# Packing the 16-row leftovers of a hybrid attention block into TensorE column groups

## The chip, the cores and the metric

One NeuronCore of one Trainium2 chip (trn2). The metric is the device time of one execution in microseconds; lower is better. The kernel is one program on one core, and everything is float32.

## The reference, cut to what matters

A decoder block: layer norm of 16 meta tokens and 2048 real tokens, then two groups of heads side by side (4 retention heads of 128, 8 forgetting-attention heads of 64), an output projection, and a mixture of 64 experts. Only the real tokens are returned.

```python
h = concatenate([meta, x])                      # 16 + 2048 = 2064 rows of 1024
h = layer_norm(h, ln0_g, ln0_b)
proj = h @ w_in                                 # rq, rk, rv, rg (4 x 128 each), fq, fk, fv (8 x 64), ff (8)
logf = log_sigmoid(ff + b_forget)
ret  = retention(rotary(rq), rotary(rk) * 128 ** -0.5, rv)      # in chunks of 128, state carried over
ret  = head_norm(ret) * silu(rg)
fox  = forgetting_attention(fq, fk, fv, logf)   # softmax(q k / 8 + c_q - c_k), c = cumsum(logf)
h = layer_norm(ALPHA * h + concatenate([ret, fox]) @ w_out, ...)
# then the mixture of experts and the last norm
```

2064 rows are sixteen blocks of 128 and 16 rows over. Two parts of the kernel meet such a leftover of 16 rows: the forgetting attention's values `fv`, in blocks from row 0, whose last block has 16 rows; and each retention head, whose first chunk is the 16 meta rows, for which only keys and values are needed (for the state), no queries and no gate.

## The kernel before, in words

The program runs in stages on one core. The **embedding stage** (`embed_phase`) normalises the rows, transposes them to `hT` (1024 features as 8 chunks of 128 partitions, 2064 columns), and on the way projects the values block by block (`values(b)`, lines 447 to 455): 8 matmuls, one for each feature chunk, stationary `hT` (128 x rows), moving the weights `wv` (128 x 512). For the last block, `b == NB - 1`, there are 16 stationary columns, and the result stands in partitions 0 to 15 of PSUM bank 7. TensorE's order at the end is: `forget()` (lines 457 to 469), `values(15)`, `values(16)`. `forget()` projects the 8 forget gates for 2048 rows in four matmuls per chunk, each of 512 rows, whose outputs start at partitions 0, 32, 64 and 96. ScalarE copies the values to SBUF (`copy_v`, line 410), and SyncE stores them to `v_rows` (line 287). ScalarE and VectorE make the gates out of `forget()`'s result: lines 366 to 380 on VectorE, 402 and 404 on ScalarE; SyncE stores the sums as `ck` (line 285), and only then, in its queue, the last value block. ScalarE copies value blocks 15 and 16 behind its part of the gates.

Then comes **retention** (`retention_phase`), a hardware loop of two rounds with two heads each. TensorE waits before its loop for the copy of value block 15 (`v_copied` at 16) and for the forget copies; ScalarE waits before its loop for all stores of the embedding stage. In a head, TensorE's `project(m)` (line 704) makes queries, keys, values and gates of chunk m (m = 0: the 16 meta rows, keys and values only, 256 columns; m > 0: 128 rows, 512 columns), in two PSUM banks by turns; ScalarE's `evacuate(m)` (lines 598 to 603) copies them out, VectorE's `rotate(m)` (lines 638 to 642) applies the rotary factors to queries and keys, and TensorE's `outer(m)` (line 714) multiplies rotated keys with weighted values into the state. The order at the start of a head is written out by hand:

```python
project(0)
project(1)
outer(0)      # waits for rotate(0)
project(2)
for n in range(NX): ...
```

After its 16 chunks a head is normalised: POOL takes the reciprocal root, VectorE subtracts and scales (line 677, 16 instructions) and multiplies with the gates (line 682), and only after that, in its program order, rotates chunk 0 of the next head. The forgetting attention (`fox_phase`) and the expert stage (`moe_phase`) follow. The attention's product of weights and values (line 1120) writes two heads to partitions 0 to 63 and 64 to 127 of one bank.

In SBUF the copy's tiles `vst` (values), `qk` (queries and keys), `vz` (weighted values) and `r` (rotated) exist twice, by turns.

Of the kernel before, what the change touches and what calls it, by code (L numbers as in the profile page):

```python
# [14 lines left out]
P = 128  # L15
D = 1024
DC = D // P
SEQ = 2048
NX = SEQ // P
META = 16  # L20
TOK = META + SEQ
NB = -(-TOK // P)
# [174 lines left out]
def embed_phase(nc, ps, ident, hT, square, x, meta, ln_g, ln_b, ln_gcol, ln_bcol, w_in, b_forget, h_rows, v_rows, ck, rope, retc, ahead):  # L197


    with Phase(nc, "emb") as ph:  # L200
# [194 lines left out]
        @block.scalar  # L395
        def _(act):
            act.wait_ge(const, 48)

            def softplus(k):
                lo, hi, _ = CUT[k]  # L400
                act.wait_ge(gate, k + 1)
                nc.scalar.activation(t2[:, lo:hi], t1[:, lo:hi], ACT.Exp).then_inc(gate_e, 1)
                act.wait_ge(gate_e, k + 1)
                nc.scalar.activation(t1[:, lo:hi], t2[:, lo:hi], ACT.Ln, bias=1.0).then_inc(gate_a, 1)

            def copy_v(b):
                act.wait_ge(v_done, b + 1)
                if b >= 2:
                    act.wait_ge(v_out[b % 2], 16 * (b // 2))
                nc.scalar.copy(vst[b % 2][0:vrows[b], :], ps[0:vrows[b], 7 if b == NB - 1 else 4 + b % 2, :]).then_inc(v_copied, 1)  # L410

            for i in range(NT):
                r = rows[i]
                act.wait_ge(turned, i + 1)
                for c in range(4):
                    ins = nc.scalar.activation(hT[:, c, tok0[i]:tok0[i] + r],
                                               ps[:, 2 * (i % 2), c * P:c * P + r], ACT.Identity,
                                               bias=bcol[:, c:c + 1], scale=gcol[:, c:c + 1])
                ins.then_inc(hT_a, 1)
                if i >= 2:  # L420
                    copy_v(i - 2)
            act.wait_ge(const_r, 48)
            for k, (o, n) in enumerate(FCH):
                act.wait_ge(f_done, 1 if n == BANK else 2)
                bank = ps[32 * k:32 * k + FH, 6, :] if n == BANK else ps[0:FH, 7, :]
                nc.scalar.activation(z[:, o:o + n], bank[:, 0:n], ACT.Identity, bias=bf[:, 0:1]).then_inc(f_copied, 1)
            softplus(0)
            copy_v(NT - 2)
            copy_v(NT - 1)

        @block.tensor
        def _(pe):
            def turn(i):
                r = rows[i]
                pe.wait_ge(normed, i + 1)
                if i >= 2:
                    pe.wait_ge(hT_a, i - 1)
                    pe.wait_ge(hT_d, i - 1)
                for c in range(DC):
                    ins = pe.transpose(ps[:, 2 * (i % 2) + c // 4, (c % 4) * P:(c % 4) * P + r],  # L440
                                       xn[i % 2][0:r, c * P:(c + 1) * P], ident[0:r, 0:r])
                ins.then_inc(turned, 1)

            def values(b):

                pe.wait_ge(hT_a, min(b + 2, NT))
                pe.wait_ge(hT_d, min(b + 2, NT))
                if b == NB - 1:
                    pe.wait_ge(f_copied, len(FCH))
                elif b >= 2:  # L450
                    pe.wait_ge(v_copied, b - 1)
                for c in range(DC):
                    ins = pe.matmul(ps[0:vrows[b], 7 if b == NB - 1 else 4 + b % 2, :], hT[:, c, P * b:P * b + vrows[b]], wv[:, c, :],
                                    start=(c == 0), stop=(c == DC - 1))
                ins.then_inc(v_done, 1)

            def forget():
                pe.wait_ge(wf_in, 16)
                pe.wait_ge(hT_a, NT)
                pe.wait_ge(hT_d, NT)  # L460
                for c in range(DC):
                    for k in range(4):
                        ins = pe.matmul(ps[32 * k:32 * k + FH, 6, :], wf[:, c, :], hT[:, c, BANK * k:BANK * (k + 1)],
                                        start=(c == 0), stop=(c == DC - 1))
                ins.then_inc(f_done, 1)
                for c in range(DC):
                    ins = pe.matmul(ps[0:FH, 7, 0:TOK - 4 * BANK], wf[:, c, :], hT[:, c, 4 * BANK:TOK],
                                    start=(c == 0), stop=(c == DC - 1))
                ins.then_inc(f_done, 1)

            pe.wait_ge(const, 48)
            for i in range(NT):
                turn(i)
                if i == 2:
                    pe.wait_ge(wv_in, 16)
                if i >= 2:
                    values(i - 2)
            forget()
            values(NT - 2)
            values(NT - 1)  # L480
# [3 lines left out]
def retention_phase(nc, ps, ident, hT, square, w_in, retc, v_rows, ck, mixed, ahead):  # L484


    with Phase(nc, "ret") as ph:
# [85 lines left out]
        @block.scalar  # L573
        def _(act):

            for sem_, n_ in ahead.rows_out:
                act.wait_ge(sem_, n_)
            act.wait_ge(w_in_s[0], 80 + START)
            with act.Fori(0, RH // 2) as j:
                for u in range(2):  # L580
                    def evacuate(m):

                        b, n = (u + m) % 2, META if m == 0 else P
                        bank = ps[0:n, b, :]
                        act.wait_ge(proj, (j * 2 + u) * NM + m + 1 + START)

                        if m == 2:
                            act.wait_ge(state_mm, (j * 2 + u) * NX + 1 + START)
                        if m >= 3:
                            act.wait_ge(att, (j * 2 + u) * NX + m - 2 + START)  # L590
                        if m == 0:
                            act.wait_ge(w_in_s[u], j * 80 + 80 + START)

                            act.wait_ge(att, (j * 2 + u) * NX + START)
                            act.sem_inc(spare[0], 1)
                        zeta = rc[u][0:n, P + 3:P + 4] if m == 0 else rc[u][:, P:P + 1]
                        if m > 0:
                            nc.scalar.activation(qk[b][:, 0:RD], bank[:, 0:RD], ACT.Copy, scale=rc[u][:, P + 1:P + 2])
                            nc.scalar.copy(v[b][:, :], bank[:, 2 * RD:3 * RD])
                        nc.scalar.copy(qk[b][0:n, RD:2 * RD], bank[:, RD:2 * RD])  # L600
                        ins = nc.scalar.activation(vz[b][0:n, :], bank[:, 2 * RD:3 * RD], ACT.Copy, scale=zeta)
                        if m > 0:
                            ins = nc.scalar.activation(sg[u][:, m - 1, :], bank[:, 3 * RD:4 * RD], ACT.Silu)
                        ins.then_inc(evac, 1)


                    act.wait_ge(mix_out[u], j * 16 + START)
                    act.sem_inc(spare[0], 1)
                    evacuate(0)
                    evacuate(1)  # L610
                    evacuate(2)
                    for n in range(NX):
                        m = n + 1
                        act.wait_ge(turned, (j * 2 + u) * NX + n + 1 + START)
                        nc.scalar.copy(rT[n % 2][:, :], ps[:, 2, 0:2 * RD]).then_inc(turned_c, 1)
                        act.wait_ge(att, (j * 2 + u) * NX + n + 1 + START)
                        nc.scalar.copy(ret[u][:, n, :], ps[:, 4 + n % 2, 0:RD]).then_inc(out_c, 1)
                        if m + 2 < NM:
                            evacuate(m + 2)
# [66 lines left out]
        def _(pe):  # L686
            pe.wait_ge(ahead.v_copied[0], ahead.v_copied[1] - 1)
            pe.wait_ge(*ahead.f_copied)
            with pe.Fori(0, RH // 2) as j:
                for u in range(2):  # L690
                    def project(m):
                        n, t0 = (META, 0) if m == 0 else (P, META + P * (m - 1))
                        b = (u + m) % 2
                        lo, hi = (RD, 3 * RD) if m == 0 else (0, 4 * RD)
                        if m < 2:

                            if u == 1:
                                pe.wait_ge(evac, (j * 2 + u) * NM + m - 1 + START)
                            else:
                                pe.wait_ge(evac, j * (2 * NM) + START)  # L700
                        else:
                            pe.wait_ge(evac, (j * 2 + u) * NM + m - 1 + START)
                        for c in range(DC):
                            ins = pe.matmul(ps[0:n, b, lo:hi], hT[:, c, t0:t0 + n], wr[u][:, c, lo:hi],  # L704
                                            start=(c == 0), stop=(c == DC - 1))
                        ins.then_inc(proj, 1)
# [1610 lines left out]
```

## Time and profile before

| | us |
|---|---|
| median of 3 runs | 3263.11 (3262.07 to 3263.48) |
| the profiled execution | 3265.91 |
| its span, first to last instruction | 3264.1 |
| TensorE busy | 3111.6 (95%) |
| VectorE, ScalarE, GpSimd busy | 1105.6, 693.6, 635.4 |
| mean granted TensorE clock | 0.982 |

How to read it. TensorE is `PE`, its weight loads `PEld`; VectorE is `DVE`, ScalarE `ACT`, GpSimd `POOL`, SyncE's DMA queue `SPq`. A row of a timeline gives start, length, engine, line, operation, what is written and read (partitions x elements), how many records in a row, and in brackets how long the engine stood idle before it and what ended that. An fp32 matmul leaves two records. The length of a merged row runs to the end of its last record, which overlaps the next row a little; the spacing of records is therefore taken from starts. `128*16 128x256` is a stationary tile of 128 partitions by 16 columns, and a moving tile of 256 columns. The granted clock is 1.00 at 2.4 GHz and 0.50 at 1.2 GHz.

### The profile page before, as it was taken

To read this page: it belongs to the slowest core of one execution; us is meant where nothing else is said; L and a number is where in the kernel's file an instruction comes from. 1 tells how busy PE (TensorE), PEld (TensorE's weight loads), DVE (VectorE), ACT (ScalarE), POOL (GpSimd) and SP (SyncE) were. 2 spreads that over 40 slices of the span, in tenths; PEclk is the share of its full clock that TensorE was granted. 3 is DMA by queue.
4 is the path that set the end of the run, shared out by engine and by line. 5 is a ranking of instruction groups with operands and counts; after the bars stand their busy time and mean duration, and the time that the engine had idled before them with its cause. 6 is when DMAs were issued, how large, how long until landed. Compare 5 with 4: busy or idle time off the path is not lost.

```text
span 3264.1 us, 38644 instructions
## 1 busy us (share of the span) xinstructions
PE 3111.6 (95%) x14302; PEld 1998.4 (61%) x14302; DVE 1105.6 (34%) x3356; ACT 693.6 (21%) x1547; POOL 635.4 (19%) x623
## 2 busy tenths in 40 slices
PE   8999999999999899898999999999999999999991
PEld 4444545454445555554556767778777778787771
DVE  6423333330035656663777331111111111111115
ACT  2221111110024454451111001111111111111114
POOL 3200000000000010101444202222222222223224
PEclk9999999999999999999999999999999999999996
DMA  6421010001000102005334467788888888888886
GB/s 227 139 66 40 1 41 1 14 12 47 20 1 8 48 9 104 11 8 179 130 123 139 140 226 210 230 238 239 233 245 244 242 240 258 261 263 270 271 262 226
DMA packets 179985, 462.06 MB, mean 142 GB/s; under 512 B 25040, under 2 KB 97568, under 8 KB 154056
## 3 DMA queue, kind: packets, MB, share of 16 engines
q1 hardware_dynamic: 134736, 342.38, 29.8%
q0 software_dynamic: 42752, 108.72, 15.2%
q10 hardware_dynamic: 2304, 8.39, 0.6%
q8 instruction: 120, 1.97, 0.2%
q14 instruction: 73, 0.60, 0.1%
HBM read 345.47 MB, written 113.92 MB: 141 GB/s over the span
## 4 chain that ended last, share of the span: by engine, by line
PE 52%; DVE 1%; DMA 0%; POOL 0%; ACT 0%; issue 0%; SPq 0%; POOLq 0%; ACTq 0%; DVEq 0%
PE ps L2229 22%; PE ps L2167 11%; PE ps L2053 7%; PE ps L2151 4%; PE ps L2099 3%; PE ps L2111 2%; PE ps L2164 2%; PE ps L2073 1%; PE ps L2063 0%; POOL moe_fin L1904 0%; DMA moe_fin<-base_rows 0%; DVE moe_fin L1617 0%; PE ps L2040 0%; DMA base_rows<-moe_yo,index 0%; DVE moe_shift L1612 0%
## 5 line engine op out<-in xcount | busy, mean ns | idle before, releaser
L704 PE MATMUL ps<-ret_w,hT 128*128 128x512 f32 (+1 forms) x1088 | 467.9, 584 | 3.2 <-issue 3.2
L2229 PEld LDWEIGHTS ps<-moe_xT,moe_wg 128*128 128x128 f32 x2048 | 352.6, 196 | 44.8 <-issue 40.8
L2229 PE MATMUL ps<-moe_xT,moe_wg 128*128 128x192 f32 (+22 forms) x2048 | 378.4, 338 | 0.0
L2229 PE MATMUL ps<-moe_xT,moe_wu 128*128 128x192 f32 (+22 forms) x2048 | 375.3, 336 | 0.0
L2167 PE MATMUL ps<-moe_wd,moe_hh 128*128 128x512 f32 (+12 forms) x800 | 366.5, 601 | 1.0 <-DVE moe_hh L1433 0.8
L2229 PEld LDWEIGHTS ps<-moe_xT,moe_wu 128*128 128x128 f32 x2048 | 353.3, 196 | 4.3
L704 PEld LDWEIGHTS ps<-ret_w,hT 128*128 128x128 f32 (+1 forms) x1088 | 196.2, 185 | 229.7 <-issue 224.1
L1840 POOL DMA_INDIRECT base_rows<-moe_yo,index x100 | 164.8, 1648 | 848.0 <-DVE moe_yo L1535 680.5
L1433 DVE TENSOR_TENSOR moe_hh<-moe_sl,ps 128x256 f32<-128x256 f32 (+19 forms) x144 | 53.8, 374 | 797.4 <-ACT moe_sl L1934 797.3
L2167 PEld LDWEIGHTS ps<-moe_wd,moe_hh 128*128 128x128 f32 (+12 forms) x800 | 136.6, 181 | 159.4 <-issue 149.8
L1058 PE MATMUL ps<-hT,fox_w 128*128 128x512 f32 (+1 forms) x576 | 228.4, 558 | 0.0
L1934 ACT ACTIVATE moe_sl<-ps 128x256 f32<-128x256 f32 (+19 forms) x144 | 49.9, 346 | 791.0 <-PE ps L2229 652.2
L910 DVE CUSTOM_DVE_ANT_0 hT<-ps,fox_c 128x512 f32<-128x512 f32 (+7 forms) x320 | 166.3, 560 | 124.5 <-PE ps L1069 124.3
L887 POOL TENSOR_TENSOR fox_diag<-fox_c,fox_causal 128x128 f32<-128x128 f32 x128 | 55.8, 458 | 700.4 <-DVE fox_mx L916 700.0
L1058 PEld LDWEIGHTS ps<-hT,fox_w 128*128 128x128 f32 x576 | 105.2, 191 | 123.3 <-issue 123.3
L1535 DVE TENSOR_SCALAR moe_yo<-ps,weight 128x512 f32<-128x512 f32 x100 | 75.0, 750 | 302.3 <-PE ps L2167 302.3
L1088 PE MATMUL ps<-ident,hT 128*128 128x128 f32 (+1 forms) x1024 | 150.7, 282 | 24.5 <-ACT hT L1011 11.1
L1011 ACT ACTIVATE hT<-hT,fox_nm 128x1936 f32<-128x1936 f32 (+15 forms) x128 | 155.0, 1212 | 69.0 <-DVE fox_nm L925 68.7
L1088 PEld LDWEIGHTS ps<-ident,hT 128*128 128x128 f32 (+1 forms) x1024 | 107.5, 137 | 87.1 <-issue 63.3
L1819 POOL DMA_INDIRECT moe_xg<-t_rows,index x129 | 129.7, 1006 | 145.7 <-DMA base_rows<-moe_yo 69.5
L2151 PEld LDWEIGHTS ps<-ident,moe_xg 128*128 128x128 f32 (+14 forms) x1032 | 131.2, 196 | 40.5 <-issue 40.1
L1113 PE MATMUL ps<-fox_pT,fox_v 128*64 128x256 f32 (+2 forms) x1088 | 144.3, 382 | 3.2 <-DVE fox_pT L938 2.8
(246 smaller groups left out, 3587.8 us busy)
## 6 DMA issues: line engine op xcount, KB each, us to landing
moe_wg<-in_we_gate SPq DMA_DIRECT2D x64, 1024.0 KB, 5.0
moe_wu<-in_we_up SPq DMA_DIRECT2D x64, 1024.0 KB, 7.1
moe_wd<-in_we_down SPq DMA_DIRECT2D x64, 1024.0 KB, 7.8
fox_c<-ck SPq DMA_DIRECT2D x8, 1032.0 KB, 8.6
emb_xin<-in_x SPq DMA_DIRECT2D x16, 512.0 KB, 3.7
h_rows<-emb_hr SPq DMA_DIRECT2D x16, 512.0 KB, 2.8
ret_w<-in_w_in SPq DMA_DIRECT2D x16, 512.0 KB, 6.6
moe_yt<-h_rows SPq DMA_DIRECT2D x16, 512.0 KB, 4.9
```

The costliest lines, as they stand in the source:

```text
L704: ins = pe.matmul(ps[0:n, b, lo:hi], hT[:, c, t0:t0 + n], wr[u][:, c, lo:hi], start=(c == 0), stop=(c == DC - 1))
L910: ins = dve.tensor_tensor_reduce(out=row[:, lo:m], in0=bank[:, 0:m - lo], in1=negc[p % 2][:, a, lo:m], scale=1.0, scalar=NEG, op0=ALU.add, ...
L1011: nc.scalar.activation(row, row, ACT.Exp, bias=nm[(2 * n + q) % 4][:, a:a + 1], accum_out=rs[n % 2][:, r:r + 1]).then_inc(exped, 1)
L1058: ins = pe.matmul(ps[:, x % 8, 0:n], wqk[job % 2][:, c, :], hT[:, c, tok:tok + n], start=(c == 0), stop=(c == DC - 1))
L1088: ins = pe.transpose(ps[0:hi - lo, T0 + g % 2, P * r:P * (r + 1)], prob[n % 2][2 * q + a][:, lo:hi], ident[:, :])
L1113: ins = pe.matmul(ps[FD * a:FD * (a + 1), O0 + n % 2, P * q0:QT], vp[p % 2][0:m, st, FD * a:FD * (a + 1)], pT[g % 4][0:m, 2 * a + q0:2 * a ...
L1819: pool.indirect_dma_start(out=xg[r][0:n, :], out_offset=None, in_=t_rows, in_offset=bass.IndirectOffsetOnAxis(ap=route.index[0:n, k * NE + ...
L1840: pool.indirect_dma_start(out=base_rows, out_offset=bass.IndirectOffsetOnAxis(ap=route.index[0:n, c:c + 1], axis=0), in_=yo[r][0:n, :], in ...
L2053: ins = pe.matmul(ps[:, 2 + a, :], mT[i % 2][:, c, :] if c < RH else fT[i % 2][:, c - RH, :], wo[:, c, a * BANK:(a + 1) * BANK], start=(c ...
L2151: ins = pe.transpose(ps[:, h, c * P:c * P + n], xg[g % NXG][0:n, 4 * h + c:D:DC], ident[0:n, 0:n])
L2167: ins = pe.matmul(ps[0:n, bank + h, :], hh[i % 2][:, f, k * P:k * P + n], rhs, start=(f == 0), stop=(f == FC - 1))
L2229: ins = pe.matmul(out, w[:, c, f:FF:FC], xT[u][:, c, 0:n], start=(c == 0), stop=(c == DC - 1))
```

## The change

The values of the last 16 rows are made in four column groups: for each feature chunk four matmuls of 128 weight columns each, whose outputs start at partitions 0, 32, 64 and 96 of bank 7, and ScalarE gathers them with four copies. The keys of the 16 meta rows are made apart from their values: keys go to partitions 32 to 47 of the bank, values stay at 0 to 15, two matmuls of 128 columns in place of one of 256; ScalarE reads the keys from there. No wait, no DMA and no other instruction is changed.

```diff
@@ embed_phase, ScalarE: copy_v
-                nc.scalar.copy(vst[b % 2][0:vrows[b], :], ps[0:vrows[b], 7 if b == NB - 1 else 4 + b % 2, :]).then_inc(v_copied, 1)
+                if b < NB - 1:
+                    ins = nc.scalar.copy(vst[b % 2][0:vrows[b], :], ps[0:vrows[b], 4 + b % 2, :])
+                else:
+                    for g in range(4):
+                        ins = nc.scalar.copy(vst[b % 2][0:vrows[b], P * g:P * (g + 1)],
+                                             ps[32 * g:32 * g + vrows[b], 7, P * g:P * (g + 1)])
+                ins.then_inc(v_copied, 1)
@@ embed_phase, TensorE: values
+                n = vrows[b]
                 for c in range(DC):
-                    ins = pe.matmul(ps[0:vrows[b], 7 if b == NB - 1 else 4 + b % 2, :], hT[:, c, P * b:P * b + vrows[b]], wv[:, c, :],
-                                    start=(c == 0), stop=(c == DC - 1))
+                    rows_c = hT[:, c, P * b:P * b + n]
+                    if b < NB - 1:
+                        ins = pe.matmul(ps[0:n, 4 + b % 2, :], rows_c, wv[:, c, :], start=(c == 0), stop=(c == DC - 1))
+                    else:
+                        for g in range(4):
+                            ins = pe.matmul(ps[32 * g:32 * g + n, 7, P * g:P * (g + 1)], rows_c, wv[:, c, P * g:P * (g + 1)],
+                                            start=(c == 0), stop=(c == DC - 1))
                 ins.then_inc(v_done, 1)
@@ retention_phase, ScalarE: evacuate
-                        nc.scalar.copy(qk[b][0:n, RD:2 * RD], bank[:, RD:2 * RD])
+                        keys = bank if m > 0 else ps[32:32 + META, b, :]
+                        nc.scalar.copy(qk[b][0:n, RD:2 * RD], keys[:, RD:2 * RD])
@@ retention_phase, TensorE: project
-                        lo, hi = (RD, 3 * RD) if m == 0 else (0, 4 * RD)
+                        hi = 3 * RD if m == 0 else 4 * RD
...
                         for c in range(DC):
+                            if m == 0:
+                                pe.matmul(ps[32:32 + n, b, RD:2 * RD], hT[:, c, t0:t0 + n], wr[u][:, c, RD:2 * RD],
+                                          start=(c == 0), stop=(c == DC - 1))
+                            lo = 2 * RD if m == 0 else 0
                             ins = pe.matmul(ps[0:n, b, lo:hi], hT[:, c, t0:t0 + n], wr[u][:, c, lo:hi],
                                             start=(c == 0), stop=(c == DC - 1))
```

In TensorE's program, from the last value blocks to the first wait of the second stage, this stood before (each row one instruction or a run of them; shapes are the output's):

```order
L453 MATMUL ps<-emb_wv,hT 128x512 [waits emb_v_copied0,emb_hT_d0,emb_hT_a0]
L453 MATMUL ps<-emb_wv,hT 128x512 x7
L453 MATMUL ps<-emb_wv,hT 16x512 [waits emb_f_copied0,emb_hT_d0,emb_hT_a0]
L453 MATMUL ps<-emb_wv,hT 16x512 x7
L685 UNCONDITIONAL_BRANCH
L689 UNCONDITIONAL_BRANCH [waits emb_f_copied0,emb_v_copied0]
L689 ISA
L700 ISA [waits ret_ret_w0]
L704 MATMUL ps<-ret_w_52,hT 16x256 [waits ret_evac]
L704 MATMUL ps<-ret_w_52,hT 16x256 x7
L704 MATMUL ps<-ret_w_52,hT 128x512 [waits ret_evac]
```

and this now:

```order
L465 MATMUL ps<-emb_wv,hT 16x128 [waits emb_f_copied0,emb_hT_d0,emb_hT_a0]
L465 MATMUL ps<-emb_wv,hT 16x128 x31
L698 UNCONDITIONAL_BRANCH
L702 UNCONDITIONAL_BRANCH [waits emb_f_copied0,emb_v_copied0]
L702 ISA
L713 ISA [waits ret_ret_w0]
L718 MATMUL ps<-ret_w_52,hT 16x128 [waits ret_evac]
L721 MATMUL ps<-ret_w_52,hT 16x128
L718 MATMUL ps<-ret_w_52,hT 16x128
L721 MATMUL ps<-ret_w_52,hT 16x128
```

Eight matmuls of 512 columns became 32 of 128, and eight of 256 became 16 of 128, keys and values by turns; the waits stand where they stood.

In ScalarE's program, at the end of the embedding stage, before:

```order
L404 ACTIVATE emb_t_92<-emb_t_93 8x2064 [waits emb_gate_e0]
L410 COPY emb_vst_81<-ps 128x512 [waits emb_v_out1,emb_v_done0]
L410 COPY emb_vst_80<-ps 16x512 [waits emb_v_out0,emb_v_done0]
L573 UNCONDITIONAL_BRANCH
L579 UNCONDITIONAL_BRANCH [waits emb_v_out1,emb_v_out0,emb_c_out0,emb_h_out1,ret_ret_w0,emb_h_out0,emb_hrow0]
```

and now:

```order
L404 ACTIVATE emb_t_92<-emb_t_93 8x2064 [waits emb_gate_e0]
L411 COPY emb_vst_81<-ps 128x512 [waits emb_v_out1,emb_v_done0]
L414 COPY emb_vst_80<-ps 16x128 [waits emb_v_out0,emb_v_done0]
L414 COPY emb_vst_80<-ps 16x128 x3
L585 UNCONDITIONAL_BRANCH
L591 UNCONDITIONAL_BRANCH [waits emb_v_out1,emb_v_out0,emb_c_out0,emb_h_out1,ret_ret_w0,emb_h_out0,emb_hrow0]
```

One copy became four; the wait for the stores still follows them.

## Rows read from the trace of the kernel before

**Rows 1.** the page: busy times, and the granted TensorE clock in 40 slices
```profile
PE 3111.6 (95%) x14302; PEld 1998.4 (61%) x14302; DVE 1105.6 (34%) x3356; ACT 693.6 (21%) x1547; POOL 635.4 (19%) x623
...
PEclk9999999999999999999999999999999999999996
```

**Rows 2.** timeline, TensorE, 132 to 166 us: start, length, line, operation [idle before]
```profile
132.94 7.05 PE L463 MATMUL ps<-hT,emb_wf 128*8 128x512 f32 x64
139.81 0.56 PE L467 MATMUL ps<-hT,emb_wf 128*8 128x16 f32 x16
140.29 14.11 PE L453 MATMUL ps<-emb_wv,hT 128*128 128x512 f32 x32
154.23 10.68 PE L704 MATMUL ps<-ret_w,hT 128*16 128x256 f32 x32
165.49 0.48 PE L714 MATMUL ps<-ret_vz,ret_r 16*128 16x128 f32 x2 [0.58 <-DVE ret_r L642]
```

**Rows 3.** timeline of ScalarE, 150 to 166 us
```profile
150.63 0.56 ACT L410 COPY emb_vst<-ps 128x512 f32<-128x512 f32 x1
...
162.41 1.28 ACT L600 ACT_TABLE_LOAD   x1 [7.40 <-DMA v_rows<-emb_vst]
...
163.86 0.35 ACT L601 ACTIVATE ret_vz<-ps,ret_rc 16x128 f32<-16x128 f32 x1
```

**Rows 4.** timeline of SyncE's DMA queue, 150 to 166 us
```profile
158.82 0.29 SPq L285 DMA_DIRECT2D ck<-emb_t  x1
159.15 0.32 SPq L287 DMA_DIRECT2D v_rows<-emb_vst  x1
```

**Rows 5.** timeline of VectorE, 150 to 166 us
```profile
157.57 1.22 DVE L380 TENSOR_SCALAR emb_t<-emb_t 8x2064 f32<-8x2064 f32 x1
...
165.15 0.21 DVE L642 TENSOR_TENSOR ret_r<-ret_cosd,ret_sind 16x64 f32<-16x64 f32 x1
```

**Rows 6.** timeline of TensorE, 1374 to 1380 us, in the forgetting attention
```profile
1378.20 1.09 PE L1120 MATMUL ps<-fox_pT,fox_v 128*64 128x128 f32 x16
1379.23 1.13 PE L1069 MATMUL ps<-fox_k,fox_q 64*128 64x512 f32 x4
```

**Rows 7.** timeline of TensorE, 286 to 316 us, into the second head
```profile
293.76 11.39 PE L704 MATMUL ps<-ret_w,hT 128*16 128x256 f32 x32
306.07 0.48 PE L714 MATMUL ps<-ret_vz,ret_r 16*128 16x128 f32 x2 [0.92 <-DVE ret_r L642]
```

**Rows 8.** timeline of VectorE, 286 to 316 us, the same place
```profile
302.73 2.29 DVE L682 TENSOR_TENSOR ret_ret<-ret_ret,ret_sg 128x2048 f32<-128x2048 f32 x1
```

**Rows 9.** timeline of TensorE, 578 to 591 us, into the fourth head
```profile
578.06 10.69 PE L704 MATMUL ps<-ret_w,hT 128*16 128x256 f32 x32
590.28 0.48 PE L714 MATMUL ps<-ret_vz,ret_r 16*128 16x128 f32 x2 [1.53 <-DVE ret_r L642]
```

**Rows 10.** timeline of TensorE, 437 to 451 us, into the third head
```profile
437.67 12.80 PE L704 MATMUL ps<-ret_w,hT 128*16 128x256 f32 x32 [3.16 <-issue]
450.40 0.48 PE L714 MATMUL ps<-ret_vz,ret_r 16*128 16x128 f32 x2
```

**Rows 11.** timeline of VectorE, 443 to 448 us, the same place
```profile
443.34 2.29 DVE L682 TENSOR_TENSOR ret_ret<-ret_ret,ret_sg 128x2048 f32<-128x2048 f32 x1
...
447.28 0.21 DVE L642 TENSOR_TENSOR ret_r<-ret_cosd,ret_sind 16x64 f32<-16x64 f32 x1
```

**Rows 12.** timeline of TensorE, 1484 to 1512 us, at the start of the MoE phase
```profile
1499.19 1.09 PE L2040 MATMUL ps<-ident,moe_mix 128*128 128x128 f32 x4 [5.81 <-PEq L145]
```

**Rows 13.** windows: stretch, its length, busy time of each engine, PEclk, DMA share, GB/s
```profile
291.70:295.10 3.40, 3.24 (x10) 1.94 (x11) 1.05 (x5) 0.37 (x2) 0.15 (x1) 0.51 0.07 10
...
431.70:441.90 10.20, 6.58 (x19) 2.91 (x18) 4.14 (x17) 0.91 (x3) 3.21 (x2) 0.50 0.65 168
...
1499.20:1506.90 7.70, 7.03 (x11) 3.20 (x12) 1.18 (x10) 0.59 (x1) 4.41 (x7) 0.50 0.83 260
...
588.70:597.00 8.30, 6.77 (x18) 3.25 (x18) 3.00 (x14) 1.13 (x5) 0.00 (x0) 1.00 0.43 126
```

## The prediction

> **What bounds the kernel now.** I read the page first: TensorE is busy 95% of the span, with the granted clock full nearly throughout [rows 1]. So TensorE time that is saved normally comes off the end; the question is whether it is saved where TensorE is the engine others wait for. The change sits in five places only: the last 16 value rows, and the 16 meta rows at the start of each of the four heads. I then read, for each of the five, the TensorE timeline and whatever ends TensorE's next wait.
>
> *Into the first head.* TensorE ends the forget projections, then does the last two value blocks (32 records from 140.29; the last 16 are the 16-row block), the meta rows' projection and the first 128 rows' projection (32 records from 154.23), and then stops for 0.58 us before the first state product, outer(0), at 165.49 [rows 2]. What ends that stop is a chain that does not begin at TensorE's late work: VectorE finishes the gate sums at 158.79; SyncE issues the store of ck and then, behind it, the store of the last 16 value rows (159.15) [rows 4, 5]; ScalarE stands 7.40 us until that store has landed, loads its table at 162.41 and copies the meta rows' keys and values by 164.21 [rows 3]; VectorE rotates the keys by 165.36 [rows 5]; outer(0) follows. The gate sums depend on the forget projections, which come before everything the change touches.
>
> *Into the second and fourth heads.* TensorE stops again in front of outer(0), 0.92 and 1.53 us, for the rotated keys [rows 7, 9]. VectorE is late there because it still finishes the previous head: the gating multiply ends at 302.73 + 2.29 = 305.02 and the rotation can only follow [rows 8].
>
> *Into the third head* it is the other way round: the keys are ready at 447.49, and TensorE reaches outer(0) at 450.40 without a stop [rows 10, 11]. Here TensorE is the late one, by 2.9 us.
>
> **The change, part by part.** An fp32 matmul is two records in this trace, so 8 matmuls of 512 columns are 16 records.
>
> *Values of the last 16 rows.* Before: (154.23 − 140.29) / 32 = 0.436 us a record, 7.0 us for the block's 16. Now 64 records of 128 columns in four column groups. Do groups overlap? The forget projections already use four groups: 64 records of 512 columns in 139.81 − 132.94 = 6.87 us, 0.107 us each against 0.436 alone, so four do run at once [rows 2]. With 128 columns the data would take a quarter, 0.027 us; the smallest spacing shown is (140.29 − 139.81) / 16 = 0.030 us [rows 2]. The dearer bound is the two-group product of the attention with 128 columns, (1379.23 − 1378.20) / 16 = 0.064 us [rows 6]. I take 0.030, nearest in groups and in load width: 64 × 0.030 = 1.9 us, saving 5.1 us (bounds: 2.9 at 0.064, 5.1 at 0.030).
>
> *Meta rows.* Before, 16 records of 256 columns, 16 × 0.436 / 2 = 3.5 us. Now 32 records of 128 columns in two groups. The nearest row is the 0.064 us of [rows 6]: 32 × 0.064 = 2.05 us, saving 1.4 us a head. Bounds: 1.7 us if pairs overlap fully, 0 if they don't.
>
> The Trainium skill (TensorEngine Tiling (Array Packing), section Key Properties) says that a change of tiling mode drains the engine, which speaks against short packed stretches between full-width ones. The row at such a switch shows 0.08 us of overlap and no gap (139.81 + 0.56 = 140.37 against a next start at 140.29) [rows 2]. If a drain did cost the 0.17 us by which the record at 154.23 is overlapped by the one before, twice in a head, the gain of a head would be 1.1 and not 1.4 us.
>
> *ScalarE's four copies in place of one.* They come behind the copy at 150.63, which is not touched. The nearest row, 16 partitions by 128, takes 0.35 us, so four end by 151.19 + 1.4 = 152.6; the store they feed stands behind ck's on SyncE until 159.15 [rows 3, 4]. Nothing, with 6.5 us of cover; without it 1.4 less the one copy now, 0.8 us at most. The keys' copy only reads other partitions: nothing. No DMA is added or moved.
>
> *What reaches the end.* **First head: no gain.** TensorE ends the values at 147.3 + 1.9 = 149.2 and now stops first for the value copy before its loop, which ScalarE ends at 150.63 + 0.56 = 151.19 [rows 3]. Then 2.05 and 16 × 0.436 = 7.0 us of projections, to 160.3. outer(0) stays at 165.49, because ScalarE's wait for the store is unchanged. The stop of 0.58 us becomes about 5.2 us: saved work of 6.5 us turns into standing. **Second and fourth: no gain**; the stops grow from 0.92 to 2.3 and from 1.53 to 2.9 us. **Third: 1.4 us gained**, covered by the 2.9 us that the keys are early.
>
> *What the longer stops cost.* TensorE's clock is the unshown part. After the stop of 5.81 us at the start of the MoE phase, TensorE works 7.7 us at 0.50 of the clock, the 1.2 GHz level [rows 12, 13]: 3.85 us lost. After the short stops at the end of the first head it works 3.4 us at 0.51: 1.7 us [rows 13]. After the third head's back edge, with a 3.16 us stop, the level is 0.50 for a stretch of 10.2 us [rows 10, 13]. And the 1.53 us stop before the fourth head was followed by a full clock [rows 13]. So for the new stops: at least 0, at most 3.85 us each. For the first head, 5.2 us of stop, I take one short stretch on the path, 1.7 us; for the 2.3 and 2.9 us stops, which lie between that row and the 3.16 us one, 1.2 us each. The projection that follows is on the path: the other engines wait for TensorE inside a head. Sum: 4.1 us.
>
> The Trainium skill (TensorE: Matmul & The Clock Gate, section Why this matters for your kernels) warns that idle gaps between bursts of matmuls bring the engine back to half rate; by that rule the second sum below is wrong and the first right. This trace agrees for the 5.81 and 3.16 us stops.
>
> **Sum:** −1.4 + 4.1 = +2.7 us. The profiled execution took 3265.9 us (span 3264.1 and 1.8 around it), so 3268.6 for such an execution; the median of the runs is 2.8 us lower, 3263.1, so the forecast is **3265.8 us**. About 0.2% (6.5 us) is what a measurement of this kernel can tell from no change, so this counts as "no change".
>
> **The rivals.**
> - *The clock stays up* at the new stops. Then only the third head counts: −1.4, 3261.7 us. For it: the 1.53 us stop that did no harm. Against it: three half-clock stretches behind or around stops [rows 12, 13]. Chance 0.27.
> - *The groups don't overlap* with 128 columns, so the change doesn't do what it says: each record 0.107 us (a quarter of 0.436), 64 of them 6.8 us and 32 of them 3.4 us, as now. 3263.1 us. Against it: the 0.064 us records [rows 6]. Chance 0.06.
> - *Slower:* each of the three new stops ends like the 5.81 us one. 3 × 3.85 = 11.6 less 1.4 is +10.2, 3273.3 us. It decides once a stop costs 2.65 us on average (3 × 2.65 − 1.4 = 6.5). For it: the level stayed low 7.7 us after that stop. Against it: the 3.4 us stretch at the first head's end, and stops half as long in two heads. Chance 0.07.
> - *Faster:* the waits I call fixed are TensorE's own. If outer(0) moves with the projections in every head, all of it counts: 5.1 + 4 × 1.4 = 10.7, 3252.4 us. For it: TensorE is busy 95% and the stops were short, at most 1.53 us. Against it: ScalarE's wait on the store and VectorE's gating multiply, neither of which begins at the changed matmuls. Chance 0.05.
>
> **How the numbers follow.** The forecast has 0.55. The range runs from the third head's best gain with no loss, 1.7, and 0.9 more for the spread of runs (the lowest shown is 1.0 below the median): 3263.1 − 2.6 = 3260.5, up to one 3.85 and two 1.7 us losses less 1.1 (+6.2, 3269.3). That takes in the "clock stays" and "no overlap" cases; left out are the slower and the faster rival, 0.12, and tails. Faster by over 0.2% (below 3256.6): 0.05. Slower (above 3269.6): 0.08, the slower rival and a tail. Within: 0.87.
>
> **What would show it.** In the profile after: 64 records of the value line in about 1.9 us; meta pairs in about 2.05 us; outer(0) of the first head still near 165.5 with a stop of about 5 us before it, and a stop of about 2 us before the first meta projection; ScalarE's wait on the value store unchanged at its end, 162.4; stops of 2.3 and 2.9 us into heads two and four; the third head about 1.4 us shorter; records at half clock right behind the long stops. If outer(0) of the first head comes before 163, the forecast is wrong on the faster side; if the clock is low for more than 5 us behind several stops, on the slower side.

## The result, and the profile after

| | before | after |
|---|---|---|
| median of 22 runs each, us | 3261.16 | 3266.33 |
| lowest and highest, us | 3255.89, 3266.33 | 3260.73, 3273.48 |
| the profiled execution, us | 3265.91 | 3271.97 |
| its span, us | 3264.1 | 3270.1 |
| TensorE busy, us | 3111.6 | 3110.0 |
| mean granted clock | 0.982 | 0.979 |

The ratio of the times is 1.0018, with a 95% interval of 1.0011 to 1.0025: the kernel that packs its leftovers is 5.2 us slower by the medians, 0.16%. (The ratio is not the quotient of the two medians, which is 1.0016; nor are the ratios further down.) The page of the kernel after answers to [rows 1]:

```profile
PE 3110.0 (95%) x14414; PEld 2004.4 (61%) x14414; DVE 1105.6 (34%) x3356; ACT 693.9 (21%) x1550; POOL 635.3 (19%) x623
...
PEclk9999999999999999999999999999999999999996
```

Busy time hardly tells: TensorE has less to do and is busy about as long. At this scale the clock row shows nothing either. The places must be looked at one by one. Into the first head, the timeline of TensorE after, as in [rows 2] (start, length, line, operation, count, idle before and its releaser):

```profile
147.50 1.94 PE L465 MATMUL ps<-emb_wv,hT 128*16 128x128 f32 x64
151.68 0.28 PE L718 MATMUL ps<-ret_w,hT 128*16 128x128 f32 x1 [2.23 <-ACT emb_vst L411]
...
154.60 7.69 PE L721 MATMUL ps<-ret_w,hT 128*16 128x128 f32 x17
165.76 0.78 PE L731 MATMUL ps<-ret_vz,ret_r 16*128 16x128 f32 x2 [3.46 <-DVE ret_r L655]
166.47 10.10 PE L721 MATMUL ps<-ret_w,hT 128*128 128x512 f32 x16
```

The packed values take 1.94 us instead of 7.0. Then TensorE stops 2.23 us for the copy of value block 15, and 3.46 us before outer(0), which starts at 165.76 where it was 165.49. Behind it project(2), line 721, takes 10.10 us; the same work took 7.13 us at this place before:

```profile
165.90 7.13 PE L704 MATMUL ps<-ret_w,hT 128*128 128x512 f32 x16
```

ScalarE and SyncE's queue after, as in [rows 3, 4]:

```profile
151.25 1.06 ACT L414 COPY emb_vst<-ps 16x128 f32<-16x128 f32 x4
162.56 1.28 ACT L613 ACT_TABLE_LOAD   x1 [10.25 <-PE ps L721]
```

```profile
158.97 0.29 SPq L285 DMA_DIRECT2D ck<-emb_t  x1
159.30 0.32 SPq L287 DMA_DIRECT2D v_rows<-emb_vst  x1
```

The four copies are there, 1.06 us in all, and end 7 us before the store that needs them is issued. ScalarE again loads its table at 162.56, 0.15 us from where it did. (The profile now puts this wait down to `PE ps L721` and not to the store. In order_after, one of the runs below whose program is the same up to here, it puts the same wait, 10.26 us, down to `DMA v_rows<-emb_vst`, so I read it as still the store's.)

The rows of the other three heads after, as in [rows 7, 9, 10]:

```profile
309.62 0.79 PE L731 MATMUL ps<-ret_vz,ret_r 16*128 16x128 f32 x2 [2.63 <-DVE ret_r L655]
310.33 9.85 PE L721 MATMUL ps<-ret_w,hT 128*128 128x512 f32 x16
...
444.39 0.39 PE L718 MATMUL ps<-ret_w,hT 128*16 128x128 f32 x1 [3.41 <-issue]
...
455.48 0.48 PE L731 MATMUL ps<-ret_vz,ret_r 16*128 16x128 f32 x2
...
595.92 0.79 PE L731 MATMUL ps<-ret_vz,ret_r 16*128 16x128 f32 x2 [2.38 <-DVE ret_r L655]
596.64 10.05 PE L721 MATMUL ps<-ret_w,hT 128*128 128x512 f32 x16
```

Stops of 2.63 and 2.38 us into the second and fourth heads, project(2) again 9.85 and 10.05 us; and between the third head's first matmul and outer(0) 455.48 − 444.39 = 11.09 us, where it was 450.40 − 437.67 = 12.73. The windows (stretch, length, busy times with records of TensorE, weight loads, VectorE, ScalarE and GpSimd, PEclk, DMA share, GB/s) of the four stretches behind the new stops:

```profile
152.00:155.40 3.40, 3.40 (x31) 2.58 (x27) 3.37 (x2) 0.30 (x2) 0.00 (x0) 0.50 0.21 77
...
165.60:172.40 6.80, 6.64 (x9) 3.02 (x10) 1.61 (x8) 1.26 (x2) 0.00 (x0) 0.50 1.17 331
309.00:315.80 6.80, 6.18 (x9) 2.87 (x10) 2.04 (x10) 0.00 (x0) 0.00 (x0) 0.50 0.55 157
595.70:602.50 6.80, 6.58 (x9) 3.02 (x10) 1.69 (x8) 0.00 (x0) 0.00 (x0) 0.50 0.55 157
```

TensorE works at the 1.2 GHz level in each of them, for 3.4 us behind the first stop and 6.8 us behind each of the three stops before outer(0).

**Where the time went.** The forgetting attention's first matmul, before and after:

```profile
718.93 16.65 PE L1058 MATMUL ps<-hT,fox_w 128*128 128x512 f32 x35
```

```profile
727.29 12.96 PE L1075 MATMUL ps<-hT,fox_w 128*128 128x512 f32 x28
```

727.29 − 718.93 = 8.4 us later. From rows: project(2) is 3.0, 2.7 and 2.9 us longer in heads one, two and four, outer(0) 0.3 us longer in each (0.78 or 0.79 against 0.48), sum 9.5; the third head's start gives back 1.6. 9.5 − 1.6 = 7.9; the remaining 0.5 us is a net of small things (the loop's back edge took 3.41 and not 3.16 us).

The clock is also low in places that nobody edited. At the end of each head TensorE stands 1.43, 0.56 and 0.46 us for ScalarE and VectorE, and half-clock stretches begin there in both kernels: before at 291.8, 431.7 and 715.0 us, after at 295.2, 438.6, 582.0 and 725.3. They fall differently from kernel to kernel, and where the next wait is another engine's, as into heads two and four, part of them vanishes in it. By the start of the MoE phase the distance is 6.2 us:

```profile
1505.36 1.09 PE L2057 MATMUL ps<-ident,moe_mix 128*128 128x128 f32 x4 [5.81 <-PEq L145]
```

against 1499.19 [rows 12]. The 2.2 us between are given back in the attention, which the change doesn't touch (more on this where the prediction is gone through).

### The profile page after: what moved, and what is told of

Read it like the earlier page. It is cut to its first block, busy times and chain, and to the rows that moved or that the text cites. A ratio compares the mean times of both kernels' runs of the same rounds, so it can differ in the third digit from the quotient of the medians.

```text
span 3270.1 us, 38871 instructions
## 1 busy us (share of the span) xinstructions
PE 3110.0 (95%) x14414; PEld 2004.4 (61%) x14414; DVE 1105.6 (34%) x3356; ACT 693.9 (21%) x1550; POOL 635.3 (19%) x623
## 4 chain that ended last, share of the span: by engine, by line
PE 52%; DVE 1%; DMA 0%; POOL 0%; ACT 0%; issue 0%; SPq 0%; POOLq 0%; ACTq 0%; DVEq 0%
PE ps L2246 22%; PE ps L2184 11%; PE ps L2070 7%; PE ps L2168 4%; PE ps L2116 3%; PE ps L2128 2%; PE ps L2181 2%; PE ps L2090 1%; PE ps L2080 0%; POOL moe_fin L1921 0%; DVE moe_fin L1634 0%; DMA moe_fin<-base_rows 0%; PE ps L2057 0%; DMA base_rows<-moe_yo,index 0%; DVE moe_shift L1629 0%
## 5 line engine op out<-in xcount | busy, mean ns | idle before, releaser
L721 PE MATMUL ps<-ret_w,hT 128*128 128x512 f32 (+1 forms) x1088 | 472.2, 590 | 0.0
L721 PEld LDWEIGHTS ps<-ret_w,hT 128*128 128x128 f32 (+1 forms) x1088 | 201.3, 190 | 222.0 <-issue 221.8
```

## The experiments

Theory: the saved matmuls stood in front of waits that TensorE doesn't set, so the work turned into stops, and the clock is low behind the stops. Rivals: packed matmuls, or the switch between packed and full-width ones, cost the time themselves; the values were on the path. Each run was measured beside the kernel before, whose median was 3261.26 us for the first four and 3261.53 for the last three. As a cleaner measure than the total I give the start of the forgetting attention in the profiled execution (before 718.93, changed kernel 727.29), since everything that was edited lies ahead of it. It is one execution for each kernel, and a half-clock stretch of 3.4 us more or less moves it by 1.7 us, so a difference of 2 or 3 us between two such starts has to be followed to its place before it means anything.

**values_only.** The values packed, the meta rows as before: of the diff, only the two pieces of the embedding stage.

> Only the values of the last 16 rows are packed; the meta rows stay as before. Theory (stops bring the clock down): TensorE stops about 2.2 us before its loop, then 7 + 3.5 us of projections end near 162, so it stops again for about 3.7 us before outer(0) of the first head; the clock falls there and the first head is 1.7 to 3.4 us longer, the other three as before (124.1 us from first to last outer). Sum +1.7 to +3.4 us. Rival (the packed meta matmuls themselves, or the switch between packed and full-width ones, cost the time): no more than 1 us from before, since only one packed stretch is left. Rival (the last value block was on the path): 5 us faster.

Measured: 3262.88 us, ratio 0.9997 (0.9988 to 1.0006); attention from 721.96. TensorE's timeline:

```profile
147.75 1.94 PE L465 MATMUL ps<-emb_wv,hT 128*16 128x128 f32 x64
151.93 12.37 PE L716 MATMUL ps<-ret_w,hT 128*16 128x256 f32 x32 [2.24 <-ACT emb_vst L411]
165.90 0.48 PE L726 MATMUL ps<-ret_vz,ret_r 16*128 16x128 f32 x2 [1.59 <-DVE ret_r L654]
166.31 8.83 PE L716 MATMUL ps<-ret_w,hT 128*128 128x512 f32 x16
```

Stops of 2.24 and 1.59 us (the second shorter than expected, since the projections of line 716 took 12.37 us and not 10.68, at a low clock behind the first stop), outer(0) where it was, and a project(2) of 8.83 us, 1.7 longer. The 5 us of saved work are worth nothing: the rival that they were on the path falls. The rival that packed matmuls cost the time foresaw no more than 1 us here, and the total doesn't exclude it. In this profile the fourth head has an 8.83 us project(2) as well:

```profile
592.13 0.48 PE L726 MATMUL ps<-ret_vz,ret_r 16*128 16x128 f32 x2 [1.52 <-DVE ret_r L654]
592.54 8.83 PE L716 MATMUL ps<-ret_w,hT 128*128 128x512 f32 x16
```

Its stop, 1.52 us, is that of the kernel before, which had no low clock behind it. So the same stop can go either way, and only 1.7 of the 3.0 us by which the attention comes later belong to the edited first head. In the total the effect is too small to be told from none: the interval excludes the upper end of what I expected, +3.4, and not the lower, +1.7.

**meta_only.** The meta rows packed, the values as before.

> Only the meta rows' keys and values are packed; the values stay at 512 columns. Theory (stops): the stop before outer(0) is 2.3 us in the first head, 2.6 in the second, about 3 in the fourth; a low clock behind each that it brings down, 1.7 to 3.4 us each; the third head gains 1.7 us. Sum between +1 and +8 us, near +4. Rival (packing is free and the clock is no matter): 1.7 us faster. Rival (values were the costly part): no change.

Measured: 3264.08 us, ratio 1.0010 (1.0001 to 1.0019), +2.8 us by the medians; attention from 723.73.

```profile
165.61 0.78 PE L719 MATMUL ps<-ret_vz,ret_r 16*128 16x128 f32 x2 [2.39 <-DVE ret_r L643]
166.32 10.03 PE L709 MATMUL ps<-ret_w,hT 128*128 128x512 f32 x16
...
309.39 0.48 PE L719 MATMUL ps<-ret_vz,ret_r 16*128 16x128 f32 x2 [2.65 <-DVE ret_r L643]
309.80 7.13 PE L709 MATMUL ps<-ret_w,hT 128*128 128x512 f32 x16
...
592.50 0.79 PE L719 MATMUL ps<-ret_vz,ret_r 16*128 16x128 f32 x2 [2.51 <-DVE ret_r L643]
593.22 9.06 PE L709 MATMUL ps<-ret_w,hT 128*128 128x512 f32 x14
```

Stops of 2.39, 2.65 and 2.51 us. Behind the first and the third project(2) takes about 10 us (the last row shows only the 14 records that lie in the view; all 16 take 9.92), behind the second 7.13. Three stops within a third of a microsecond of each other, with both outcomes: one stop cost nothing, the others about 3 us. What decides between them no run here shows; I treat it as chance. That is what the range from +1 to +8 had to allow for; "packing is free and the clock no matter", 1.7 us faster, falls. The rival that the values were the costly part (no change) lies only just outside the interval; against it speak the two long project(2).

**filled.** Everything packed, and the packed matmuls repeated, so that TensorE works as long as before.

```diff
-                for c in range(DC):
+                for c in [c for rep in range(4 if b == NB - 1 else 1) for c in range(DC)]:
                     rows_c = hT[:, c, P * b:P * b + n]
...
-                        for c in range(DC):
+                        for c in [c for rep in range(2 if m == 0 else 1) for c in range(DC)]:
                             if m == 0:
```

> As the changed kernel, but the packed values are computed four times over and the packed meta projection twice, so that TensorE works as long at these places as before the change. Theory (stops): stops back to about 0.6, 0.9 and 1.5 us, each head 124.1 us from first to last outer, total within 1 us of before, so about 4 to 5 us faster than the changed kernel although it does more work. Rival (packed matmuls or the mode switch cost it): the loss of the changed kernel stays or grows, 5 us or more above before.

Measured: 3259.10 us, ratio 0.9995 (0.9986 to 1.0004); attention from 718.62, 8.7 us before the changed kernel's.

```profile
147.37 7.18 PE L465 MATMUL ps<-emb_wv,hT 128*16 128x128 f32 x256
...
157.96 2.41 PE L721 MATMUL ps<-ret_w,hT 128*128 128x512 f32 x5
...
165.62 0.48 PE L731 MATMUL ps<-ret_vz,ret_r 16*128 16x128 f32 x2 [0.53 <-DVE ret_r L655]
166.03 7.13 PE L721 MATMUL ps<-ret_w,hT 128*128 128x512 f32 x16
...
591.04 0.48 PE L731 MATMUL ps<-ret_vz,ret_r 16*128 16x128 f32 x2 [1.47 <-DVE ret_r L655]
```

```profile
165.50:172.30 6.80, 6.68 (x17) 3.22 (x18) 1.59 (x7) 2.15 (x5) 0.00 (x0) 1.00 1.17 332
...
592.00:598.80 6.80, 6.80 (x19) 3.17 (x18) 0.57 (x3) 0.10 (x1) 0.00 (x0) 1.00 0.40 114
```

256 packed records in 7.18 us, the stops back to 0.53 and 1.47, and the clock at 1.00 behind them. (Into the second head there was no stop at all, where I expected 0.9: TensorE had come late, from 6.8 us at half clock at the end of the first head.) By the medians this is 7.2 us under the changed kernel, where I expected 4 to 5. With four times the packed values and twice the packed meta rows the loss is gone. So neither packing nor switching costs it: the rival, a loss of 5 us or more, falls.

**short_values.** Nothing packed, but the last value block is made from two of eight feature chunks, so the last 16 value rows are partial sums.

```diff
+                last = DC // 4 if b == NB - 1 else DC
-                for c in range(DC):
+                for c in range(last):
```

> The kernel before with no packing at all, but the last value block's projection uses only two of its eight feature chunks (the last 16 value rows are thus partial sums): 4 records of 512 columns, 1.7 us, about as long as the packed block's 1.9. Theory (stops): the same stops and the same low clock in the first head as with packed values alone, +1.7 to +3.4 us although work is left out. Rival (packing costs it): no change, since nothing is packed.

Measured: 3262.43 us, ratio 1.0003 (0.9994 to 1.0012); attention from 721.24.

```profile
151.51 12.37 PE L705 MATMUL ps<-ret_w,hT 128*16 128x256 f32 x32 [2.28 <-ACT emb_vst L410]
165.47 0.48 PE L715 MATMUL ps<-ret_vz,ret_r 16*128 16x128 f32 x2 [1.59 <-DVE ret_r L643]
165.87 8.83 PE L705 MATMUL ps<-ret_w,hT 128*128 128x512 f32 x16
```

Row for row the picture of packed values alone: 2.28 and 1.59 us of stop, 12.37 us of projections, 8.83 us of project(2). Three quarters of a block's work left out, nothing packed, and the first head's project(2) is longer by the same 1.7 us. (Here too the fourth head's stop of 1.52 us was followed by a project(2) of 8.83.) Only the stops are common to the two. In the total both are within noise of before, so the experiment rests on the trace: +1.7 to +3.4 us was expected, and the medians differ by 1.2.

**order_after, order_before, order_meta.** If TensorE stands in front of outer(0) for the rotated keys, project(2), which only needs the meta rows' bank copied out, can go ahead of it. In the changed kernel, in the kernel before, and with the meta rows packed but the values not:

```diff
                     project(1)
-                    outer(0)
                     project(2)
+                    outer(0)
```

> The changed kernel with project(2) ahead of outer(0) in the order of a head. Theory (TensorE stands in front of outer(0) while project(2) could run): in heads two to four project(2) needs only the copy of the meta rows, done some 6 us earlier, so there is no stop before it and no low clock behind it; the packed work of heads two to four comes off (3 x 1.7 us) together with the old stops (0.9 and 1.5 us). First head: project(2) waits for that copy, done at 164.2, so a stop of about 2 us stays, and one fall of the clock (1.7 to 3.4 us). Sum: about -7.5 -1.3 + 2.5 = -6 us against before. Rival (VectorE's chain sets the start of the head whatever TensorE does): outer(0) later by 7 us than now and the chunk loop starts later with it, so no gain, or a loss up to 5 us.

> The kernel before, nothing packed, with project(2) ahead of outer(0). Theory: the stops of 0.9 and 1.5 us into heads two and four go, and project(2) of the first head starts about 1.2 us sooner: -3 to -4 us against before. Rival (as above): no gain or a loss.

> Meta rows packed, values not, and project(2) ahead of outer(0). Theory: the unpacked values keep TensorE busy until 154.2, so the first head's stop before project(2) is only about 1.3 us and the clock mostly stays up; the other heads as in the first of these runs. -3.5 - 5.1 = about -8 us against before, the fastest of the three. Rival (the stop is harmless and the values should have been packed): the same time as the first of these runs, or slower than it.

| | median, us | ratio to before (3261.53) | attention from |
|---|---|---|---|
| order_after | 3257.14 | 0.9982 (0.9973 to 0.9991) | 714.20 |
| order_before | 3256.89 | 0.9988 (0.9979 to 0.9997) | 713.75 |
| order_meta | 3255.43 | 0.9978 (0.9969 to 0.9987) | 710.36 |

All three beat both kernels: their intervals lie below 1 and the changed kernel's above it. The order alone brings 4.6 us by the medians (expected 3 to 4); order_after is 4.4 us under before (expected 6). outer(0) of the first head does come later, at 171.63 us in order_before, and the kernel is faster all the same: the rival that VectorE's chain sets the start of a head falls. The first head of order_after, and of order_meta:

```profile
164.45 8.83 PE L721 MATMUL ps<-ret_w,hT 128*128 128x512 f32 x16 [3.87 <-ACT ret_vz L614]
173.21 0.48 PE L731 MATMUL ps<-ret_vz,ret_r 16*128 16x128 f32 x2
```

```profile
164.36 7.13 PE L709 MATMUL ps<-ret_w,hT 128*128 128x512 f32 x16 [1.18 <-ACT ret_vz L602]
171.42 0.48 PE L719 MATMUL ps<-ret_vz,ret_r 16*128 16x128 f32 x2
```

With everything packed there is a stop of 3.87 us, where I expected about 2, and project(2) behind it takes 8.83 us; with the values unpacked the stop is 1.18 us and project(2) takes 7.13. Into the second head of order_meta there is no stop at all:

```profile
299.72 8.32 PE L709 MATMUL ps<-ret_w,hT 128*128 128x512 f32 x19
307.96 0.48 PE L719 MATMUL ps<-ret_vz,ret_r 16*128 16x128 f32 x2
...
308.65 7.03 PE L709 MATMUL ps<-ret_w,hT 128*128 128x512 f32 x16
```

The packed meta rows now shorten the way to the attention by 713.75 − 710.36 = 3.4 us, of the 5.1 expected. Of the rest, 0.5 us is a longer stop at the loop's back edge (3.98 against 3.45 us); and order_meta has a stretch at 0.50 from 568.9 to 575.6 us, where order_before has 1.00, against a shorter one in the third head: by the traces some 2 us more of work at half clock, so about 1 us (an estimate). In the totals order_meta is 6.1 us under before by the medians (expected 8), and its interval overlaps with those of the other two: that it beats the kernel before is shown, that it beats the other two is not. So by the totals the rival that the values should have been packed as well is not excluded.

## Why the prediction was right, point by point

**Right: where the saved work would go.** outer(0) of the first head did not move (165.49, 165.76); the stops into heads two and four grew to 2.63 and 2.38 us (forecast 2.3 and 2.9); the third head alone gained, 1.6 us (forecast 1.4). The forecast direction of the sum, slower by less than 0.2%, is what was measured: +5.2 by the medians, forecast +2.7, and 3266.33 us against a forecast of 3265.8 and a range of 3260.5 to 3269.3. Part of the closeness is luck. The forecast step was half of the measured one, and its starting point was too high. The three runs that the forecast started from had a median of 3263.1; over 22 runs it is 3261.2.

**Right: the packed durations.** 64 records in 1.94 us (forecast 1.9). For the meta rows I took 0.064 us a record; in filled, 64 of them lie between 154.4, where they start, and 157.96, (157.96 − 154.4) / 64 = 0.056, closer to full overlap. That is 32 × 0.056 = 1.8 us and a saving of 1.7 and not 1.4; the third head gained 1.6.

**Mis-sized: "What the longer stops cost", 4.1 us.** In the profiled execution it was 9.5 us, 3.3, 3.0 and 3.2 for the three heads, where I had put 1.7, 1.2 and 1.2. I had priced none above the short stretch, 3.4 us at half clock; after all three stops it was 6.8 us. outer(0) at half clock, 0.78 us and not 0.48, I had left out. By the medians, which take in executions with luckier stops, the term is 5.2 + 1.6 = 6.8 us. The bounds I gave, 0 to 3.85 each, held. The mean clock of single executions bears this out: of the changed kernel's runs, the slowest (3273.48 us) had a mean clock of 0.979 and the fastest (3260.73) 0.983. A thousandth of the clock over 3265 us is 6.5 us at the lower level and 3.3 us lost, so four are 13 us, and the two runs are 12.8 us apart.

One of the rows that the prices leaned on was misread. The prediction has the 10.2 us at half clock come after the 3.16 us stop at the loop's back edge. By its own rows the stretch begins at 431.70, and the stop at 437.67 − 3.16 = 434.51: the clock was down 2.8 us before that stop, behind the short stops at the head's end. So the row doesn't show what a stop of 3.16 us does to a full clock, and it doesn't bear out the rule on idle gaps, though the prediction says so.

The Trainium skill (TensorE: Matmul & The Clock Gate, section Why this matters for your kernels) has it that idle gaps between bursts of matmuls lead back to half rate, and the gaps it means are longer than most of the stops here. The traces show it for most of the shorter ones too, of 2.2 us and more, but not for all: not behind 2.65 us into the second head of meta_only (7.13 us of project(2)), and not behind the 2.23 us before the loop in order_after, where the clock stayed at 1.00. They show it for stops of 1.52 to 1.59 us as well, twice each in values_only and short_values, and not behind 1.53 us in the kernel before or 1.47 in filled.

**Missed: the stop before the loop also lowers the clock.** I had forecast that stop at about 2 us (2.23) and left it without a price. Behind it the projections ran at half clock for 3.4 us. It cost nothing at the end: together with a start 0.5 us later than forecast (151.68 against 151.19) it only shortened the next stop, from the forecast 5.2 to 3.46 us.

**The rivals.** "The clock stays up" (−1.4) is refuted by the windows, "the groups don't overlap" by 1.94 us for 64 records, "faster" by outer(0) at 165.76. The slower rival had the right mechanism: its 3.85 us per stop is nearer to the 3.2 us of this profile than my 1.2 to 1.7, and its threshold was 2.65 us a stop on average. The profiled execution is above that; the median of the runs is not (6.8 / 3 = 2.3).

The rule of the Trainium skill that a change of tiling mode drains the engine (TensorEngine Tiling (Array Packing), section Key Properties) shows no cost that these runs can resolve. In filled the first full-width matmul starts 157.96 − 157.76 = 0.20 us behind the last packed pair, where the pairs are 0.11 us apart; and filled switches as often as the changed kernel and loses nothing.

**The 2.2 us in the attention.** The attention took 780.3 us from its first matmul to the MoE phase's in the profile before, and 778.1 after, with no edit there. The traces put it down to TensorE: it was busy 725.9 and 723.6 us there with the same matmuls (4225 and 4226 records), 2.3 us less, and VectorE and ScalarE equally long within 0.1 us. The stretches at 0.50 in which it had work sum to about 27 us before and 22 after, and half of that difference is 2.5 us. It is the fall of the clock in these two executions and nothing that the change does by design. Why the stretches fall as they do stays open.

## What to carry to other kernels

Less work on the busiest engine is worth something only where nobody else ends its next wait: read what ends that wait, in each place that the edit touches, before counting the saving. Where the wait is another engine's, the saving becomes a stop, and on TensorE a stop of two or three microseconds can have a price of its own: here the matmuls behind it ran at the lower clock in most cases, and the kernel with some 11 us less work was 5.2 us slower. The remedy is to have other ready work in front of the wait: here one line of order, project(2) ahead of outer(0), brought 4.6 us where neither packing alone brought anything. With it the packing of the meta rows shortened the way to the attention by 3.4 us in the profiles; the totals don't tell it from the order alone.

## What the runs showed of the hardware

- Two column groups with 128 moving columns of fp32 take about 0.056 us a record, four groups 1.94 / 64 = 0.030 us. Groups overlap also across instructions that have nothing to do with each other: in meta_only the next stage's key matmuls (line 706, partitions 32 to 47) began while the last value block (line 453, partitions 0 to 15) still ran, and ahead of records of it that stand before them in TensorE's program:

```profile
152.53 0.39 PE L706 MATMUL ps<-ret_w,hT 128*16 128x128 f32 x2
152.96 1.02 PE L453 MATMUL ps<-emb_wv,hT 128*16 128x512 f32 x2
153.39 0.39 PE L706 MATMUL ps<-ret_w,hT 128*16 128x128 f32 x2
```

- Stops of nearly one length were followed by a full clock or by 3.4 or 6.8 us at half: 1.5 us with and without, 2.2 us with and without, 2.4 to 2.7 us with and without. project(2) then takes 7.13, 8.83 or about 10 us. Half-clock stretches also begin at the ends of heads, behind stops of 1.43, 0.56 and 0.46 us, in some heads and not in others (before at 431.7 us, at 1.00 from 575 to 585). By the mean clocks above, the low clock accounts, within their rounding, for the 12.8 us between the fastest and the slowest run of the changed kernel.
